# First token half ahead in the last two units of a stage, and x turned block by block in banks of its own

## Chip, cores and metric

The kernel runs on one core of a Trainium2 chip. The metric is the device time of one execution in microseconds (us). Below PE is TensorE (PEld its weight loads), ACT is ScalarE, DVE is VectorE, SP is the engine that issues most DMAs, POOL is GpSimd.

## What is computed

Two transformer blocks on 256 tokens of width 1024, all in float32. The first: a SwiGLU FFN (width 2816), an RWKV-7 mixer with a pooling branch, a second SwiGLU FFN. The second: windowed and differential attention, cross attention on a memory of 256 rows, a squared-ReLU MLP (width 4096). Each stage takes a root-mean-square norm of x, works, and adds to x:

```
x = x + 0.5 * swiglu(rms_norm(x, ffn1_norm), ffn1_w_gate, ffn1_w_up, ffn1_w_down)
h = rms_norm(x, mix_norm); p = h @ w_in
x = x + concatenate([y_rw, y_pool], axis=-1) @ w_out
x = x + 0.5 * swiglu(rms_norm(x, ffn2_norm), ffn2_w_gate, ffn2_w_up, ffn2_w_down)
x = rms_norm(x, final_norm)
...attention on x and cross attention on x and mem, then the MLP, each added to x
```

## The kernel before

**Units.** Every weight matrix is read once, in 280 units of 128x1024 elements (512 KB), numbered from the start of the program. SP loads a unit into one of three `raw` slots. ACT rounds it to a high part `whi` (`split_hi`, L1149), DVE takes the rest `wlo` (`split_lo`, L1652), each in a ring of six slots; a unit's slot is free when PE has used the unit of six before (`unit_used`). Activations are split in the same way, so PE multiplies high by high, high by low and low by high.

**Two kinds of unit.** `a_unit` produces a block of 128 outputs for all 256 tokens: for each of the 8 chunks c of the width it multiplies `XT[:, c]`, 512 columns (high and low) with `whi` and 256 with `wlo`. `b_half`, `b_unit` and `b_banks` produce 1024 outputs for 128 tokens (a token half, `tt` 0 or 1): 6 matmuls of 512 columns for one half, into banks 0 and 1 for the first half and 2 and 3 for the second. All go through the helper at L472. `b_last` is the last unit of a stage: first half, then second, with a signal (`quarter_used`) when each bank of 512 outputs is done.

**FFN.** 22 chunks of 128 hidden values. For chunk j PE computes a gate unit and an up unit (banks 4 and 6, or 5 and 7), ACT and DVE make H from them, and PE uses H in a down unit (`b_unit`). PE's order is gate and up of chunk j, then down of chunk j - 1. ACT and DVE go through `chunk(j)`, with three weight splits of later units woven in.

**A border between stages.** DVE adds the four banks to x (`update_x`, L1720 or L1722, one instruction for each quarter k: k is half and width half). PE turns x (`norm_t`, L561): 16 transposes of 128x128, two chunks of x to a bank, banks 4 to 7, in the order width half, token half. When both token halves of two chunks are there (`tp`), ACT scales and rounds them to `XT` high (`norm_hi`, L1186), then DVE takes the low part of both (`norm_lo`, L1696 and L1697) and signals `xt_ready`; the first `a_unit` of the next stage waits for `xt_ready` ahead of each second chunk. The norm itself (sum of squares, `norm_sums`, L1170, and the row scale by a matmul with a diagonal, `row_scale`) is applied later, to the outputs of the first units. Memory rows are turned in the last part of the second FFN (`norm_t("mem")`). A table of norm gains and other vectors comes in as rows, is turned by one matmul (L592) ahead of the last unit of the first FFN, and copied by DVE (L1827).

**Order.** The order of each engine's work is written out by hand; engines wait on semaphores that count events, and each engine runs its list strictly in order.

## Time and profile before

| | us |
|---|---|
| median of 3 runs | 994.62 |
| lowest, highest | 994.14, 995.46 |
| the profiled execution | 995.92 |
| its span (first to last instruction) | 994.0 |
| PE busy | 952.2 (96%) |
| PE weight loads busy | 817.2 (82%) |
| DVE busy | 664.2 (67%) |
| ACT busy | 541.2 (54%) |
| bytes read from HBM | 151.89 MB, mean 154 GB/s |

A row of the timeline gives start, duration, engine, line, operation, what is written from what, how many instructions are merged, and in brackets how long the engine was idle before and who released it. The stages are found by time: the first FFN to 202, the mixer to 373, the second FFN to 564, attention to 737, cross attention to 804, the MLP to the end.

### The profile page before, as it was taken

To read this page: it belongs to the slowest core of one execution; us is meant where nothing else is said; L and a number is where in the kernel's file an instruction comes from. 1 tells how busy PE (TensorE), PEld (TensorE's weight loads), DVE (VectorE), ACT (ScalarE), POOL (GpSimd) and SP (SyncE) were. 2 spreads that over 40 slices of the span, in tenths; PEclk is the share of its full clock that TensorE was granted. 3 is DMA by queue.
4 is the path that set the end of the run, shared out by engine and by line. 5 is a ranking of instruction groups with operands and counts; after the bars stand their busy time and mean duration, and the time that the engine had idled before them with its cause. 6 is when DMAs were issued, how large, how long until landed. Compare 5 with 4: busy or idle time off the path is not lost.

```text
span 994.0 us, 17685 instructions
## 1 busy us (share of the span) xinstructions
PE 952.2 (96%) x6228; PEld 817.2 (82%) x6228; DVE 664.2 (67%) x1101; ACT 541.2 (54%) x980; POOL 30.0 (3%) x59
## 2 busy tenths in 40 slices
PE   6999999989989999999999999998899999999997
PEld 5788888879889877888888887887888888888885
DVE  4776766577786467766667785777457366666665
ACT  6564555477545337555555676546646446554452
POOL 3002000000000001000000000002100000000000
PEclk9999999999999999999999999997999999999999
DMA  7677766545220226766656665552047136665652
GB/s 216 201 220 216 207 186 189 154 128 149 85 66 4 65 87 168 212 186 185 189 185 195 189 182 157 170 169 86 1 117 222 49 123 191 191 201 177 194 186 85
DMA packets 204177, 153.62 MB, mean 155 GB/s; under 512 B 5323, under 2 KB 189872, under 8 KB 204128
## 3 DMA queue, kind: packets, MB, share of 16 engines
q1 hardware_dynamic: 202896, 151.08, 50.9%
q0 software_dynamic: 1232, 1.87, 0.9%
q8 instruction: 32, 0.52, 0.2%
q14 instruction: 17, 0.14, 0.0%
HBM read 151.89 MB, written 1.05 MB: 154 GB/s over the span
## 4 chain that ended last, share of the span: by engine, by line
PE 84%; DVE 7%; ACT 5%; issue 2%; DMA 2%; SPq 0%; DVEq 0%; ACTq 0%
PE ps L472 83%; DVE wlo L1652 2%; ACT whi L1149 1%; DMA raw<-in_w_ckv 1%; DMA raw<-in_ffn_w_gate 1%; DVE XT L1697 1%; ACT XT L1186 0%; DMA raw<-in_w_up 0%; ACT arena L1358 0%; DVE X L1720 0%; ACT arena L1170 0%; DVE arena L1889 0%; PE ps L561 0%; DVE arena L1844 0%; ACT arena L1351 0%
## 5 line engine op out<-in xcount | busy, mean ns | idle before, releaser
L472 PE MATMUL ps<-XT,whi 128*128 128x512 f32 (+1 forms) x1584 | 521.9, 382 | 7.5 <-DVE XT L1697 7.5
L1652 DVE TENSOR_TENSOR wlo<-raw,whi 128x1024 fp32r<-128x1024 f32 x280 | 337.1, 1222 | 107.6 <-ACT whi L1149 86.6
L472 PE MATMUL ps<-XT,wlo 128*128 128x256 f32 x1440 | 404.8, 281 | 0.0
L472 PEld LDWEIGHTS ps<-XT,whi 128*128 128x128 f32 x1584 | 289.9, 189 | 69.7 <-issue 7.6
L1149 ACT ACTIVATE whi<-raw 128x1024 fp32r<-128x1024 f32 x280 | 292.4, 1054 | 53.0 <-PE ps L472 21.1
L472 PEld LDWEIGHTS ps<-XT,wlo 128*128 128x128 f32 x1440 | 273.2, 190 | 3.2
L472 PE MATMUL ps<-whi,H 128*128 128x512 f32 x608 | 177.7, 393 | 2.8 <-issue 2.5
L472 PEld LDWEIGHTS ps<-whi,H 128*128 128x128 f32 x608 | 109.0, 188 | 26.0 <-issue 2.7
L472 PE MATMUL ps<-arena 64*64 64x64 f32 (+6 forms) x1576 | 99.6, 250 | 8.6 <-DVE arena L2185 2.0
L472 PEld LDWEIGHTS ps<-arena 64*64 64x64 f32 (+3 forms) x1576 | 91.1, 153 | 16.6 <-DVE arena L2185 2.9
L472 PE MATMUL ps<-wlo,H 128*128 128x512 f32 x304 | 95.6, 393 | 0.0
L472 PEld LDWEIGHTS ps<-wlo,H 128*128 128x128 f32 x304 | 57.1, 188 | 13.3
L472 PE MATMUL ps<-whi,XT 128*128 128x512 f32 x192 | 56.1, 400 | 0.3 <-DVE XT L1696 0.3
L1211 ACT ACTIVATE arena<-ps 128x256 f32<-128x256 f32 x44 | 16.7, 380 | 58.5 <-PE ps L472 58.5
L1221 ACT ACTIVATE arena<-ps 128x256 f32<-128x256 f32 x44 | 16.9, 384 | 48.8 <-PE ps L472 48.8
L472 PEld LDWEIGHTS ps<-whi,XT 128*128 128x128 f32 x192 | 35.4, 188 | 9.3 <-issue 1.6
L1229 ACT ACTIVATE H<-arena 128x256 fp32r<-128x256 f32 x44 | 18.4, 418 | 38.5 <-DVE arena L1797 38.5
L1261 ACT ACTIVATE arena<-ps 128x256 f32<-128x256 f32 x42 | 16.0, 380 | 41.5 <-PE ps L472 41.5
L1786 DVE TENSOR_TENSOR arena<-ps,arena 128x256 f32<-128x256 f32 x44 | 18.6, 423 | 28.0 <-ACT arena L1211 27.9
L1593 ACT ACTIVATE arena<-ps 128x256 f32<-128x256 f32 x32 | 12.2, 381 | 46.0 <-PE ps L472 46.0
L1800 DVE TENSOR_TENSOR H<-arena,H 128x256 fp32r<-128x256 f32 x44 | 18.7, 426 | 24.4 <-ACT H L1229 24.4
L1597 ACT ACTIVATE H<-arena 128x256 fp32r<-128x256 f32 x32 | 13.4, 418 | 35.4 <-DVE arena L2295 35.4
(255 smaller groups left out, 713.6 us busy)
## 6 DMA issues: line engine op xcount, KB each, us to landing
raw<-in_ffn_w_gate SPq DMA_DIRECT2D x44, 512.0 KB, 4.6
raw<-in_ffn_w_up SPq DMA_DIRECT2D x44, 512.0 KB, 3.9
raw<-in_ffn_w_down SPq DMA_DIRECT2D x44, 512.0 KB, 4.7
raw<-in_w_in SPq DMA_DIRECT2D x36, 512.0 KB, 3.9
raw<-in_w_up SPq DMA_DIRECT2D x32, 512.0 KB, 4.0
raw<-in_w_down SPq DMA_DIRECT2D x32, 512.0 KB, 4.6
raw<-in_w_out SPq DMA_DIRECT2D x16, 512.0 KB, 3.5
raw<-in_w_ckv SPq DMA_DIRECT2D x16, 512.0 KB, 4.6
```

The source lines that it names most:

```text
L472: return pe.matmul(o, st, mv, start=start, stop=stop, skip_group_check=True)
L1149: act.activation(whi[:, n % RING, :], raw[:, n % RAW, :], ACT.Copy).then_inc(hi_ready, 1)
L1211: act.activation(GL[:, q, :], PS[4 + q][:, T:2 * T], ACT.Copy).then_inc(g_low, 1)
L1221: act.activation(UL[:, q, :], PS[6 + q][:, T:2 * T], ACT.Copy).then_inc(u_low, 1)
L1229: act.activation(H[:, q, 0:T], HS[:, q, :], ACT.Copy).then_inc(h_hi, 1)
L1261: act.activation(dst[:, i % 2, :], bank[:, T:2 * T], ACT.Copy).then_inc(sem_low, 1)
L1593: act.activation(UL[:, q, :], PS[4 + q][:, T:2 * T], ACT.Copy).then_inc(r_low, 1)
L1597: act.activation(H[:, q, 0:T], HS[:, q, :], ACT.Copy).then_inc(r_hi, 1)
L1652: dve.tensor_tensor(wlo[:, n % RING, :], raw[:, n % RAW, :], whi[:, n % RING, :].bitcast(F32), sub).then_inc(lo_ready, 1)
L1697: return dve.scalar_tensor_tensor(XT[:, c, T:2 * T], ps, scale, hi, mul, sub)
L1786: dve.tensor_tensor(GS[:, q, :], PS[4 + q][:, 0:T], GL[:, q, :], add).then_inc(g_raw, 1)
L1800: dve.tensor_tensor(H[:, q, T:2 * T], HS[:, q, :], H[:, q, 0:T].bitcast(F32), sub).then_inc(h_ready, 1)
```

## The change

- **Last two units.** Where a stage ends with two down units n and n + 1, PE takes the first token half of n, the first half of n + 1 (`b_banks`, both quarters signalled), the second half of n, then the second half of n + 1. This is `last_two` at the end of attention and cross attention; the mixer's end had its halves in such an order already; the FFNs are rewritten by hand. In the FFNs gate and up of chunk 21 are moved ahead of the down unit of chunk 19, loads and splits follow that order, and H of chunk 21 goes to a third slot.
- **Turning.** `turn_x(name, 0)` makes the 8 transposes of the first token half between the second half of unit n and the second half of unit n + 1; `turn_x(name, 1)` makes the other 8 after the last unit. Each transpose has a wait of its own. Chunks 0 to 3 go to banks 4 to 7, chunks 4 and 5 to banks 0 and 1, chunks 6 and 7 to the upper halves of banks 0 and 1.
- **Copy and split** go chunk by chunk: ACT signals each chunk, DVE signals each, and PE's first unit waits for each. In the shared banks ACT waits for the transposes of both chunks, and for chunks 6 and 7 also until DVE has read chunk 4 and 5. This holds at the start of the kernel too. The memory rows and the turning ahead of attention (`turn_pairs`) keep the pairs.
- **DVE.** The copy of the vector table in the first FFN is moved ahead of the last two splits of `chunk(21)`, and the transpose that it waits for behind the first half of unit 65. At the mixer's end the X updates of the first half are moved ahead of two splits.

What it makes of the order. PE at the end of attention (`whi,XT` and `wlo,XT` are the down units, `CON,X` the transposes, `XT,whi` the first unit of cross attention), before:

```order
L472 MATMUL ps<-whi,XT 128x512 x3
L472 MATMUL ps<-wlo,XT 128x512
L472 MATMUL ps<-whi,XT 128x512 x2
L472 MATMUL ps<-wlo,XT 128x512
L472 MATMUL ps<-whi,XT 128x512 x2
L472 MATMUL ps<-wlo,XT 128x512
L472 MATMUL ps<-whi,XT 128x512 x2
L472 MATMUL ps<-wlo,XT 128x512
L472 MATMUL ps<-whi,XT 128x512
L561 MATMUL ps<-CON,X 128x128 x16
L472 MATMUL ps<-XT,whi 128x512
```

and now:

```order
L486 MATMUL ps<-whi,XT 128x512 x3
L486 MATMUL ps<-wlo,XT 128x512 x2
L486 MATMUL ps<-whi,XT 128x512 x2
L568 MATMUL ps<-CON,X 128x128 x8
L486 MATMUL ps<-whi,XT 128x512
L486 MATMUL ps<-wlo,XT 128x512
L486 MATMUL ps<-whi,XT 128x512 x2
L486 MATMUL ps<-wlo,XT 128x512
L486 MATMUL ps<-whi,XT 128x512
L568 MATMUL ps<-CON,X 128x128 x8
L486 MATMUL ps<-XT,whi 128x512
```

Eight of the sixteen transposes now stand ahead of the last six matmuls. DVE at the end of the first FFN (`H` is the last chunk's, `wlo` the splits of two mixer units, `VEC` the table, `X` the updates), before:

```order
L1800 TENSOR_TENSOR H<-arena,H 128x256
L1652 TENSOR_TENSOR wlo<-raw,whi 128x1024 x2
L1827 COPY VEC<-ps 128x95
L1720 SCALAR_TENSOR_TENSOR X<-ps,SMALL,X 128x512 x4
L1697 SCALAR_TENSOR_TENSOR XT<-ps,VEC,XT 128x256 x8
```

and now:

```order
L1836 TENSOR_TENSOR H<-arena,H 128x256
L1843 COPY VEC<-ps 128x95
L1690 TENSOR_TENSOR wlo<-raw,whi 128x1024 x2
L1755 SCALAR_TENSOR_TENSOR X<-ps,SMALL,X 128x512 x4
L1735 SCALAR_TENSOR_TENSOR XT<-ps,VEC,XT 128x256 x8
```

The copy, which waits for PE, now stands ahead of both splits. DVE at the end of the mixer (numbers are the banks), before:

```order
L1652 TENSOR_TENSOR wlo<-raw,whi 128x1024 x4
L1722 TENSOR_TENSOR X<-ps0,X 128x512
L1722 TENSOR_TENSOR X<-ps1,X 128x512
L1722 TENSOR_TENSOR X<-ps2,X 128x512
L1722 TENSOR_TENSOR X<-ps3,X 128x512
```

and now:

```order
L1690 TENSOR_TENSOR wlo<-raw,whi 128x1024 x2
L1757 TENSOR_TENSOR X<-ps0,X 128x512
L1757 TENSOR_TENSOR X<-ps1,X 128x512
L1690 TENSOR_TENSOR wlo<-raw,whi 128x1024 x2
L1757 TENSOR_TENSOR X<-ps2,X 128x512
L1757 TENSOR_TENSOR X<-ps3,X 128x512
```

Two of the four splits now stand behind the updates of the first token half.

The core of the diff:

```diff
-        MEM_BANKS, T_BANKS = (4, 6, 5, 7), (4, 5, 6, 7)
+        PAIR_BANKS = {"mem": (4, 6, 5, 7), "mix2": (4, 5, 6, 7)}
+        X_BANKS = ((4, 0), (5, 0), (6, 0), (7, 0), (0, 0), (1, 0), (0, T), (1, T))
+
+        def turned_x(name, c):
+
+            if name in PAIR_BANKS:
+                bank, at = PAIR_BANKS[name][c // 2], (c % 2) * T
+            else:
+                bank, at = X_BANKS[c]
+            return PS[bank][:, at:at + T]
...
-                with sp.Fori(0, 10) as i:
+                with sp.Fori(0, 9) as i:
...
+                load(b + 57, 0, cols(u, 19 * P))
+                load(b + 58, 0, rows(d)[:, 18:19, :])
+                load(b + 59, 0, cols(g, 20 * P))
+                load(b + 60, 0, cols(u, 20 * P))
+                load(b + 61, 0, cols(g, 21 * P))
+                load(b + 62, 0, cols(u, 21 * P))
+                for j in (19, 20, 21):
+                    load(b + 44 + j, 0, rows(d)[:, j:j + 1, :])
...
-                    if after and c % 2 == 0:
-                        pe.wait_ge(xt_ready, 4 * NTP[after] + c // 2 + 1)
+                    if after:
+                        pe.wait_ge(xt_ready, KC * NTP[after] + (c - c % 2 + 2 if after in PAIR_BANKS else c + 1))
...
+            def turn_x(name, tt):
+
+                for c in range(KC):
+                    if name == "ffn1":
+                        pe.wait_ge(x_in[tt], 16)
+                    else:
+                        pe.wait_ge(x_upd, 4 * (UPD[name] - 1) + 2 * tt + c // 4 + 1)
+                    ins = pe.transpose(turned_x(name, c)[:, tt * P:(tt + 1) * P], X[:, tt, c * P:(c + 1) * P], ident)
+                    if tt == NT - 1:
+                        ins.then_inc(tp, 1)
+
+            def last_two(n, acts, name):
+
+                b_half(n, 0, acts[0], 0)
+                b_banks(n + 1, acts[1], 0, 2)
+                b_half(n, 0, acts[0], 1)
+                if name:
+                    turn_x(name, 0)
+                b_banks(n + 1, acts[1], 1, 1).then_inc(unit_used, 1)
+                if name:
+                    turn_x(name, 1)
...
-                with pe.Fori(0, 10) as i:
+                with pe.Fori(0, 9) as i:
                     for k in range(2):
                         gate_up(2 + k, 5 + 3 * k, i * 6, i * 2)
                         down(1 + k, 7 + 3 * k, i * 6, i * 2)
-                if f == 0:
+                gate_up(20, 59)
+                gate_up(21, 61)
+                down(19, 63)
+                pe.wait_ge(h_ready, J + 21)
+                if f:
+                    turn_pairs("mem", [0])
+                b_half(b + 64, 0, H[:, 0, :], 0)
+                pe.wait_ge(h_ready, J + FC)
+                b_banks(b + 65, H[:, 2, :], 0, 2)
+                if f:
+                    turn_pairs("mem", [1])
+                else:
                     pe.wait_ge(table_in, 16 * 4)
                     pe.wait_ge(rows_in, 16 * 17)
-                    pe.wait_ge(h_ready, FC)
                     pe.transpose(PS[7][:, KC:N_VEC], ROWS[0:N_VEC - KC, :],
                                  ident[0:N_VEC - KC, 0:N_VEC - KC]).then_inc(vec_tp, 1)
-                if f:
-                    norm_t("mem", [0])
-                    pe.wait_ge(h_ready, 2 * FC)
-                    norm_t("mem", [1])
-                pe.wait_ge(h_ready, J + FC)
-                b_last(b + 65, H[:, 21 % 2, :])
+                b_half(b + 64, 0, H[:, 0, :], 1)
+                if f == 0:
+                    pe.wait_ge(vec_ready, 2)
+                    turn_x("mix", 0)
+                b_banks(b + 65, H[:, 2, :], 1, 1).then_inc(unit_used, 1)
+                if f == 0:
+                    turn_x("mix", 1)
...
+                pe.wait_ge(yt_ready, 4 + 2)
+                for c in range(3):
+                    b_half(B_WOUT + 4 + c, 0, XT[:, c, :], 1)
+                turn_x("ffn2", 0)
+                b_banks(B_WOUT + 7, XT[:, 3, :], 1, 1).then_inc(unit_used, 1)
+                turn_x("ffn2", 1)
...
+                last_two(B_WOUT2 + KC - 2, [XT[:, c, :] for c in (KC - 2, KC - 1)], "cross")
...
             def norm_hi(name, gain):
-                q = NTP[name]
-                for b in range(4):
-                    act.wait_ge(tp, 4 * q + b + 1)
-                    for c in (2 * b, 2 * b + 1):
-                        bank = PS[(MEM_BANKS if name == "mem" else T_BANKS)[b]]
-                        ins = act.activation(XT[:, c, 0:T], bank[:, (c % 2) * T:(c % 2 + 1) * T], ACT.Copy,
-                            scale=vec(gain, c))
-                        if c % 2:
-                            ins.then_inc(xt_hi, 1)
+                q = KC * NTP[name]
+                for c in range(KC):
+                    if name in PAIR_BANKS:
+                        act.wait_ge(tp, q + c - c % 2 + 2)
+                    else:
+                        act.wait_ge(tp, q + (c + 1 if c < 4 else 7 + c % 2))
+                        if c >= 6:
+                            act.wait_ge(xt_ready, q + c - 1)
+                    act.activation(XT[:, c, 0:T], turned_x(name, c), ACT.Copy, scale=vec(gain, c)).then_inc(xt_hi, 1)
...
-                    n_gate, n_up = (0, 1) if j == 0 else (3 * j - 1, 3 * j)
+                    n_gate, n_up = (0, 1) if j == 0 else (61, 62) if j == 21 else (3 * j - 1, 3 * j)
+                    slot = 2 if j == 21 else q
...
             def norm_lo(name, gain):
-                q = NTP[name]
-                for b in range(4):
-                    dve.wait_ge(xt_hi, 4 * q + b + 1)
-                    for c in (2 * b, 2 * b + 1):
-                        bank = PS[(MEM_BANKS if name == "mem" else T_BANKS)[b]]
-                        ins = rest(c, bank[:, (c % 2) * T:(c % 2 + 1) * T], vec(gain, c))
-                    ins.then_inc(xt_ready, 1)
-
-            def update_x(nth, end, scale=0):
+                q = KC * NTP[name]
+                for c in range(KC):
+                    dve.wait_ge(xt_hi, q + (c - c % 2 + 2 if name in PAIR_BANKS else c + 1))
+                    rest(c, turned_x(name, c), vec(gain, c)).then_inc(xt_ready, 1)
+
+            def update_x(nth, end, scale=0, tiles=range(NT)):
 
                 if scale:
                     dve.wait_ge(fac_ready, scale)
-                for k in range(4):
+                for k in range(2 * tiles[0], 2 * tiles[-1] + 2):
...
+                        if f == 0:
+                            dve.wait_ge(vec_tp, 2)
+                            dve.tensor_copy(VEC[:, KC:N_VEC], PS[7][:, KC:N_VEC]).then_inc(vec_ready, 1)
...
-                for c in range(2, LEAD + 1 + KC - RING - 1):
-                    split_to(B_WOUT + RING + c + 1)
-                update_x(2, B_WOUT + KC)
+                split_to(B_WOUT + RING + 4)
+                update_x(2, B_WOUT + KC, tiles=[0])
+                split_to(B_WOUT + LEAD + KC)
+                update_x(2, B_WOUT + KC, tiles=[1])
```

## Rows read from the trace of the kernel before

**Rows 1.** The page, part 4: shares of the chain that ended last.
```profile
PE 84%; DVE 7%; ACT 5%; issue 2%; DMA 2%; SPq 0%; DVEq 0%; ACTq 0%
```

**Rows 2.** Timeline, attention to cross: start us, us, engine, line, operation, count [idle <-releaser].
```profile
736.65 0.39 PE L472 MATMUL ps<-whi,XT 128*128 128x512 f32 x1
...
736.88 1.91 PE L561 MATMUL ps<-CON,X 128*128 128x128 f32 x16
737.74 3.03 ACT L1186 ACTIVATE XT<-ps,VEC 128x256 fp32r<-128x256 f32 x8 [7.70 <-PE ps L561]
738.61 3.23 DVE L1697 SCALAR_TENSOR_TENSOR XT<-ps,VEC,XT 128x256 fp32r<-128x256 f32 x8 [0.84 <-ACT XT L1186]
...
739.63 0.47 PE L472 MATMUL ps<-XT,whi 128*128 128x512 f32 x1 [0.84 <-DVE XT L1697]
```

**Rows 3.** Timeline, first FFN to the mixer, PE and DVE.
```profile
198.99 0.24 PE L592 MATMUL ps<-CON,arena 95*128 95x95 f32 x1
...
199.18 2.36 DVE L1652 TENSOR_TENSOR wlo<-raw,whi 128x1024 fp32r<-128x1024 f32 x2 [0.45 <-PE ps L472]
...
201.63 2.72 DVE L1720 SCALAR_TENSOR_TENSOR X<-ps,SMALL,X 128x512 f32<-128x512 f32 x4
201.65 0.39 PE L472 MATMUL ps<-whi,H 128*128 128x512 f32 x1
...
206.39 0.47 PE L472 MATMUL ps<-XT,whi 128*128 128x256 f32 x2 [1.12 <-DVE XT L1697]
```

**Rows 4.** Timeline, mixer to the second FFN, PE and DVE.
```profile
369.81 2.59 DVE L1652 TENSOR_TENSOR wlo<-raw,whi 128x1024 fp32r<-128x1024 f32 x2 [2.75 <-ACT whi L1149]
...
372.32 0.39 PE L472 MATMUL ps<-whi,XT 128*128 128x512 f32 x1
...
376.90 0.47 PE L472 MATMUL ps<-XT,whi 128*128 128x512 f32 x1 [1.11 <-DVE XT L1697]
```

**Rows 5.** Timeline, start of the kernel, DVE, ACT and PE.
```profile
11.23 3.22 DVE L1697 SCALAR_TENSOR_TENSOR XT<-ps,VEC,XT 128x256 fp32r<-128x256 f32 x8
...
12.75 1.11 ACT L1149 ACTIVATE whi<-raw 128x1024 fp32r<-128x1024 f32 x1
...
22.07 1.06 ACT L1149 ACTIVATE whi<-raw 128x1024 fp32r<-128x1024 f32 x1 [1.65 <-DMA raw<-in_ffn_w_gate]
...
28.46 0.69 PE L472 MATMUL ps<-whi,H 128*128 128x512 f32 x2 [2.45 <-issue]
```

**Rows 6.** Timeline, the first H of the MLP, DVE and PE.
```profile
810.50 0.42 DVE L2293 TENSOR_TENSOR arena<-ps,arena 128x256 f32<-128x256 f32 x1 [0.33 <-ACT arena L1593]
...
811.93 0.43 DVE L2298 TENSOR_TENSOR H<-arena,H 128x256 fp32r<-128x256 f32 x1 [0.55 <-ACT H L1597]
...
812.71 0.63 PE L472 MATMUL ps<-whi,H 128*128 128x512 f32 x2
```

**Rows 7.** Timeline, the mixer's row scale, DVE and PE.
```profile
209.81 1.23 DVE L1652 TENSOR_TENSOR wlo<-raw,whi 128x1024 fp32r<-128x1024 f32 x1 [1.21 <-ACT whi L1149]
...
212.34 0.59 PE L472 MATMUL ps<-arena,SMALL 128*128 128x256 f32 x2
```

**Rows 8.** Timeline, end of the second FFN, DVE and PE.
```profile
559.03 0.43 DVE L1800 TENSOR_TENSOR H<-arena,H 128x256 fp32r<-128x256 f32 x1 [0.55 <-ACT H L1229]
...
560.99 0.48 PE L472 MATMUL ps<-whi,H 128*128 128x512 f32 x1
...
564.34 0.47 PE L472 MATMUL ps<-XT,whi 128*128 128x512 f32 x1 [0.35 <-DVE XT L1697]
```

**Rows 9.** Timeline, the first unit of the kernel, PE.
```profile
13.03 0.63 PE L472 MATMUL ps<-XT,whi 128*128 128x512 f32 x1
...
13.67 0.63 PE L472 MATMUL ps<-XT,whi 128*128 128x512 f32 x1
...
16.68 0.40 PE L472 MATMUL ps<-XT,whi 128*128 128x512 f32 x1
```

More of the change, by code:

```diff
@@ L492, in a_unit_summed @@
                 for c in range(KC):
-                    if after and c % 2 == 0:
-                        pe.wait_ge(xt_ready, 4 * NTP[after] + c // 2 + 1)
+                    if after:
+                        pe.wait_ge(xt_ready, KC * NTP[after] + (c - c % 2 + 2 if after in PAIR_BANKS else c + 1))
                     cs = slice(c * P, (c + 1) * P)
@@ L554, in norm_t @@
                             pe.wait_ge(mem_in, 16)
[L555 to L556 removed]
                         else:
                             pe.wait_ge(x_upd, 4 * (UPD[name] - 1) + 2 * tt + h + 1)
[L559 to L562 removed]
+                        for c in range(4 * h, 4 * h + 4):
+                            ins = pe.transpose(turned_x(name, c)[:, tt * P:(tt + 1) * P], src[:, tt, c * P:(c + 1) * P],
+                                               ident)
                             if tt == NT - 1:
[L564 removed]
+                                ins.then_inc(tp, 1)
             def ffn(b, f):
@@ L1045, in attention @@
                     last.then_inc(odt_mm, 1)
-                for c in range(KC):
+                for c in range(KC - 2):
                     pe.wait_ge(yt_ready, N_MIXED + max(4, c + 1))
-                    if c < KC - 1:
-                        b_unit(B_WOUT2 + c, 0, XT[:, c, :], start=(c == 0))
-                    else:
-                        b_last(B_WOUT2 + c, XT[:, c, :])
+                    b_unit(B_WOUT2 + c, 0, XT[:, c, :], start=(c == 0))
+                pe.wait_ge(yt_ready, N_MIXED + KC)
+                last_two(B_WOUT2 + KC - 2, [XT[:, c, :] for c in (KC - 2, KC - 1)], "cross")
             def cross():
-                norm_t("cross")
                 for i in range(KC):
@@ L1086, in cross @@
                 pe.wait_ge(sc_exp, 12 + 4)
-                for c in range(KC):
+                for c in range(KC - 2):
                     pe.wait_ge(yt_ready, N_MIXED + KC + c + 1)
-                    if c < KC - 1:
-                        b_unit(B_CO + c, 0, XT[:, c, :], start=(c == 0))
-                    else:
-                        b_last(B_CO + c, XT[:, c, :])
+                    b_unit(B_CO + c, 0, XT[:, c, :], start=(c == 0))
+                pe.wait_ge(yt_ready, N_MIXED + 2 * KC)
+                last_two(B_CO + KC - 2, [XT[:, c, :] for c in (KC - 2, KC - 1)], "mlp")
             def mlp():
```

38 lines of the change are left out of this document (8 added, 30 removed).

## The prediction

> **What bounds the kernel now.** I read the busy table and the chain of waits first: the chain lies 84% on PE and 83% on the one matmul helper, L472 [rows 1]. So the kernel is one row of matmuls, and what can be won is what stands between them where one stage ends and the next begins. I then read the timeline around each such border, engine by engine, because the chain merges the steps there. Three kinds of gap are seen. At the border from attention to cross attention PE issues its last matmul at 736.65 (done issuing .23 later, at 736.88), turns x with 16 transposes in 1.91, and issues the next matmul at 739.63: 2.75 us [rows 2]. From cross attention to the MLP the picture is the same. After the first FFN the same step takes 206.39 - 201.88 = 4.51 [rows 3], and after the mixer 376.90 - 372.55 = 4.35 [rows 4], because there the four X updates of DVE stand behind two weight splits (wlo). The start of the kernel has a wait of its own: PE idles 2.45 until 28.46, when the first H is ready [rows 5].
>
> **The new border, step by step.** Count from T, the end of the last matmul. Prices: an X update 2.72/4 = .68 [rows 3]; a copy of one chunk on ACT 3.03/8 = .38 in a row, .42 alone; a split of one chunk on DVE 3.23/8 = .40 [rows 2]; six matmuls of 512 columns 6 x .23 = 1.38 (736.65 to the next issue at 736.88) [rows 2]; eight transposes 1.91/2, so .9 without the tail [rows 2]. The sixteen transposes are no fewer, and eight of them now stand before the last six matmuls: T is .9 later. The third X update starts .19 after its quarter, which is three matmuls before T, and ends at T + .2. The first transpose of the second half goes at T + .27, ACT starts .29 later (rows 2: the sixth transpose, at 736.88 + 5 x .114 = 737.45, released ACT at 737.74), ends at T + 1.0; DVE, just through with its fourth update, splits chunk 0 until T + 1.4; PE starts at T + 1.5. Border: .9 + 1.5 = 2.4. Each transpose is now behind its own wait; the first of the sixteen stands behind one already met and follows at .23 like any other [rows 2], so I take 0 for them, and +.07 each, the lead an unhidden weight load could take, as no more than the upper end.
>
> **Attention to cross, cross to MLP.** The first matmul comes 2.75 - 2.4 = .35 earlier, but the first unit isn't bound by it. DVE hands over a chunk every .40 and PE uses it in .35 (a matmul of 512 columns at .23, one of 256 at half that), so the unit ends with DVE. Before: DVE starts at 738.61, ends 3.23 later, and PE has the two chunks of the last pair left: 738.61 + 3.23 + .06 + .70 = 742.60. Now: DVE starts at 736.88 + .9 + 1.0 = 738.78 and only one chunk is left behind it: 738.78 + 3.23 + .1 + .42 = 742.53. The .1 is the two last chunks, which share banks 0 and 1 with chunks 4 and 5, so ACT may take them only when DVE is done with those. I take **-.1** for each of the two (from -.4, if DVE gets ahead, to +.5 with the dear transposes).
> ACT ends its eight copies later, though: chunk 7 follows DVE's chunk 5, at 738.78 + 6 x .40 + .42 = 741.6 against 737.74 + 3.03 = 740.8. In the MLP ACT's next work is the hi split of a unit and DVE's the lo split behind it, and only then comes DVE's part of the first H, which had waited .33 for ACT at 810.50. H is ready there at 812.36 and PE takes it at 812.71 [rows 6], .35 of slack; DVE's three-step row (ACT 1.06, DVE 1.23) moves by .8 less that .3, so H comes at 812.9. PE waits **+.3** (0 to +.6).
>
> **Mixer to the second FFN.** Here the code does more: the first two X updates go ahead of DVE's last two splits (third pair of order excerpts), so they are over before unit 6 is. The splits end at 369.81 + 2.59 = 372.40 [rows 4], before the third quarter is ready at T - .69 = 372.76. So the border is the plain one, 2.4 for 4.35. In the unit's end: before, DVE started 1.02 before PE, as 738.61 stands before 739.63, at 375.88, unit end 375.88 + 3.23 + .76 = 379.87; now 372.55 + .9 + 1.0 = 374.45, end 374.45 + 3.23 + .1 + .42 = 378.20. **-1.7** (-2.0 to -1.2).
>
> **First FFN to the mixer.** Not so here. DVE's order is now H, VEC copy, two splits, X updates (second pair of excerpts). The copy waits for a transpose of the ROWS table that PE makes at 198.99 [rows 3] in both kernels, since the gate and up units and 24 down matmuls stand before it in both orders. Before, the splits ran from 199.18 and the copy after them; now DVE sits from its last H (some 3 us earlier, as chunk 21 is computed before unit 63) until 199.3, copies .25, splits 2.36 until 201.9 [rows 3], updates X until 202.6 and 203.3. PE is through with the half unit at 200.5 and stands: **the first turning waits for X, a new wait of 2.2 us**. Turning until 203.8, six matmuls: T = 205.2. DVE starts at T + 1.0 = 206.2 against 206.39 - 1.02 = 205.37, and the unit ends at 206.2 + 3.23 + .1 + .42 = 209.95 against 205.37 + 3.23 + .76 = 209.36: +.6. Then the row scale: PE made it at 212.34, after DVE's split at 209.81 (1.23) and .6 of scaling [rows 7], a slack of .7. This split waits for ACT, whose copies now end at 209.1 and no longer at 207.5: 1.6 later. xn so comes at 213.2 to 213.3. **+.9** (-.3, if DVE splits sooner than I think, to +1.4).
>
> **The start.** ACT went through its eight copies without DVE and began unit 1's hi split at 12.75; DVE began its chunks only at 11.23 [rows 5]. Now ACT's chunk 6 waits for DVE's chunk 4: 11.23 + 5 x .404 = 13.25, and the split follows at 14.0, 1.2 later. Behind it on ACT are the sums of squares, then splits 2 and 3; behind those on DVE the scale and lo splits; SP issues the next loads once these are done, and such a load is what ACT waited for at 22.07 (1.65) [rows 5]. The load ahead of it moves only .7, and if they share the way the delay is between .7 and 1.2. From there the first H hangs on ACT, and PE on H. PE's own start .4 earlier buys nothing, it only idles longer. **+1.0** (0, if loads and copies make it up, to +1.3).
>
> **Second FFN to the memory rows.** The turning of the memory rows has the same sixteen transposes, around another unit. H of chunk 21 was ready at 559.03 + .43 = 559.46 and PE took it at 560.99 [rows 8]. It hangs on a split and a load, so I don't let it move, while PE now wants it six matmuls and eight transposes earlier, at 560.99 - 1.38 - .8 = 558.8: a wait of .7. PE had waited .35 (.5 with the tail) for DVE at 564.34 [rows 8], which takes most of it, and the pace of DVE in that unit the rest. **+.1** (0 to +.7).
>
> **Sum.** -.1 -.1 +.3 -1.7 +.9 +1.0 +.1 = +.4 us. The profiled execution took 995.92 (span 994.0), so I expect 996.3 for one like it, and 994.62 + .4 = **995.0 for the median**; the profiled one stands 1.3 above that median with its recording, and the difference carries over.
>
> **Rivals.** (1) *The borders give what they seem to give.* If my two losses aren't there, because ACT and DVE make up for the bank waits and the splits run before the VEC copy is due, the gaps fall to 2.4 everywhere: -2.1, -1.95, -.35, -.35 = -4.75, so 989.9; with the DVE bound on the first unit kept and only the start and the first border free, -1.7 -1.4 -.2 = -3.3, 991.3. For it: 4.51 and 4.35 are real gaps [rows 3, 4]. Against: the order on DVE and the late start of its chunks at 11.23 [rows 5]. I give 15%.
> (2) *Slower, by the clock.* The wait before the first down unit grows from 2.45 to some 3.9 (mine plus the .4 of PE's earlier end). After 2.45 it held: the two matmuls at 28.46 take .69 together [rows 5], hardly more than two at full clock. If it falls to its lower level (1.2 for 2.4 GHz) there, the matmuls run as at the start, one chunk in .64 (13.03 to 13.67) for .35, until 16.68 [rows 9]: 3.65 x (1 - .35/.64) = 1.65, with the first chunk 1.8. Time 996.8. It decides only if the idle stretch is long enough, and my +1.0 comes with it. 10%.
> The Trainium skill, TensorE: Matmul & The Clock Gate, section on HAM oscillation, says that PE gaps beyond a certain length re-throttle the array and the ramp is paid again; by that page the longer wait is nearer to such a fall than the old one, and no row here shows a fall at this place.
> (3) *More waits of the small kind*: the dear transposes at all four borders (up to .07 x 16 each) and H late in both FFNs: +2 to +3, 997.2. 5%.
>
> **How the numbers follow.** Forecast, 70%: 995.0, own range 993.4 to 996.4 (the bounds of the terms don't all fall on one side). Rival 1 15%, rival 2 10%, rival 3 5%. For 8 in 10 the range goes to 992.3 below and 996.9 above. A measurement of this kernel can tell about 0.2%, here 2 us, from no change: faster means below 992.6, slower above 996.6. Faster: 13%, from rival 1 mostly. Slower: 12%, from rivals 2 and 3 and the forecast's edge. Same: 75%.
>
> **What would show it.** After the mixer: PE's gap made of eight transposes, six matmuls, eight transposes and .6 idle, the next stage 1.7 earlier. After the first FFN: PE idle for 2 us ahead of the first eight transposes, released by an X update; xn after 213. At the start: ACT waiting inside its eight copies for DVE, and PE idle for over 3 us before the first down unit at 29.4. At the two late borders: no more than .4 between old and new. Wrong it would be if PE doesn't wait for X after the first FFN, if the first H comes at 28.5 as before, or if the time is under 992.6.

## The result: about 0.3% slower

The changed kernel took 999.36 us (median of 5 executions, 999.01 to 1000.24), the kernel before 994.71 beside it (5 executions, 994.14 to 998.8): ratio 1.0033, 95% interval 1.002 to 1.0046. (The ratio is the estimate that goes with this interval; the two medians by themselves stand 1.0047 apart.) I had forecast 995.0 (992.3 to 996.9) and no change that can be told. The profiled execution of the changed kernel has a span of 997.6 us, that of before 994.0.

The chain of the changed kernel still lies on PE, 83% for 84% [rows 1]. So the 3.55 us between the two spans are to be found as steps between the same instructions of the two timelines. First the start, which answers to [rows 5]. Timeline, ACT, then PE (start us, us, engine, line, operation, count [idle <-releaser]; the helper of L472 is now L486, the copies of ACT L1226 for L1186, its hi split L1186 for L1149):

```profile
12.97 0.87 ACT L1226 ACTIVATE XT<-ps,VEC 128x256 fp32r<-128x256 f32 x2 [1.20 <-DVE XT L1735]
13.73 1.05 ACT L1186 ACTIVATE whi<-raw 128x1024 fp32r<-128x1024 f32 x1
...
22.54 1.06 ACT L1186 ACTIVATE whi<-raw 128x1024 fp32r<-128x1024 f32 x1 [1.68 <-DMA raw<-in_ffn_w_gate]
...
28.93 0.71 PE L486 MATMUL ps<-whi,H 128*128 128x512 f32 x2 [3.35 <-issue]
29.47 0.62 PE L486 MATMUL ps<-wlo,H 128*128 128x512 f32 x2
29.93 1.80 PE L486 MATMUL ps<-whi,H 128*128 128x512 f32 x4
31.53 1.05 PE L486 MATMUL ps<-wlo,H 128*128 128x512 f32 x2
```

ACT waits 1.20 for DVE ahead of its last two copies, the hi split comes at 13.73 for 12.75, and the first down unit (the first that uses H) .47 later, though the first load had landed .40 earlier here (DVE's first chunk 10.83 for 11.23): .87 counted from that load. Then four matmuls take 1.80. Busy time by windows, with the granted clock (PEclk), of the changed kernel and of before, shows why:

```profile
28.00:30.00 2.00, 1.07 (x5) 0.93 (x6) 1.15 (x2) 2.00 (x3) 0.00 (x0) 1.00 0.71 204
30.00:32.00 2.00, 2.00 (x7) 1.51 (x6) 1.97 (x3) 1.40 (x3) 0.00 (x0) 0.51 0.28 82
32.00:34.00 2.00, 2.00 (x8) 1.62 (x7) 1.96 (x4) 0.81 (x3) 0.00 (x0) 0.64 0.91 269
```
```profile
30.00:32.00 2.00, 2.00 (x12) 1.69 (x11) 1.97 (x5) 1.33 (x3) 0.00 (x0) 1.00 0.22 58
32.00:34.00 2.00, 2.00 (x13) 1.72 (x13) 1.86 (x3) 0.49 (x2) 0.00 (x0) 1.00 1.02 278
```

The third number from the right is the clock: 1.00 is 2.4 GHz, .5 is 1.2 GHz. It fell behind the wait of 3.35, at 30.0, when PE had been back at work for 1.1 us, and not behind 2.45. By 201.01, where the ROWS table is turned (198.99 before), the changed kernel is 2.02 behind: 1.55 of it for the fall.

Next the first FFN to the mixer [rows 3, 7], DVE, PE and DVE again:

```profile
197.55 0.42 DVE L1836 TENSOR_TENSOR H<-arena,H 128x256 fp32r<-128x256 f32 x1 [0.55 <-ACT H L1267]
201.29 0.26 DVE L1843 COPY VEC<-ps 128x95 f32<-128x95 f32 x1 [3.32 <-PE ps L634]
201.47 2.35 DVE L1690 TENSOR_TENSOR wlo<-raw,whi 128x1024 fp32r<-128x1024 f32 x2
203.73 1.40 DVE L1755 SCALAR_TENSOR_TENSOR X<-ps,SMALL,X 128x512 f32<-128x512 f32 x2
204.62 1.22 PE L568 MATMUL ps<-CON,X 128*128 128x128 f32 x8 [1.94 <-DVE X L1755]
...
209.02 0.47 PE L486 MATMUL ps<-XT,whi 128*128 128x256 f32 x2 [0.28 <-DVE XT L1735]
...
213.75 1.23 DVE L1690 TENSOR_TENSOR wlo<-raw,whi 128x1024 fp32r<-128x1024 f32 x1 [1.83 <-ACT whi L1186]
```

DVE stands 3.32 us for the table, PE 1.94 for X. And the mixer to the second FFN [rows 4], the one border that gained:

```profile
376.34 1.37 DVE L1757 TENSOR_TENSOR X<-ps,X 128x512 f32<-128x512 f32 x2
377.08 1.33 PE L568 MATMUL ps<-CON,X 128*128 128x128 f32 x8
...
378.59 0.47 PE L486 MATMUL ps<-XT,whi 128*128 128x512 f32 x1 [0.17 <-DVE XT L1735]
```

The whole way, as steps of the changed kernel against before (us, from the two profiles):

| stretch | step | forecast |
|---|---|---|
| first load lands | -.40 | - |
| start to the first H | +.86 | +1.0 |
| clock falls behind it | +1.55 | 0 |
| first FFN to mixer: first matmul +.61, row scale +.76 | +1.37 | +.9 |
| mixer to second FFN: first matmul -1.69, first unit +.31 | -1.38 | -1.7 |
| second FFN to memory -.10, and the rows behind -.26 | -.36 | +.1 |
| attention | -.83 | 0 |
| attention to cross: first matmul -.09, first unit +.30, behind it +.06 | +.27 | -.1 |
| clock falls in cross attention | +1.63 | 0 |
| cross to MLP: first matmul -.08, first unit +.31, first H another +.22, second H +.42 | +.87 | +.2 |

At the borders to the second FFN, to cross attention and to the MLP the first unit behind the border is .30 or .31 longer. ACT and DVE of the changed kernel at attention to cross show where from; PE starts the unit there at 740.35:

```profile
739.21 2.30 ACT L1226 ACTIVATE XT<-ps,VEC 128x256 fp32r<-128x256 f32 x6 [8.37 <-PE ps L568]
739.72 2.44 DVE L1735 SCALAR_TENSOR_TENSOR XT<-ps,VEC,XT 128x256 fp32r<-128x256 f32 x6 [0.25 <-ACT XT L1226]
741.87 0.87 ACT L1226 ACTIVATE XT<-ps,VEC 128x256 fp32r<-128x256 f32 x2 [0.35 <-DVE XT L1735]
742.37 0.88 DVE L1735 SCALAR_TENSOR_TENSOR XT<-ps,VEC,XT 128x256 fp32r<-128x256 f32 x2 [0.21 <-ACT XT L1226]
```

ACT waits .35 for DVE ahead of chunks 6 and 7, which share banks with 4 and 5, and DVE then .21 for ACT, so PE gets its last two chunks later.

The second fall of the clock stands where the two kernels do the same work behind the same wait (2.54 us in both). Timeline, PE, of the changed kernel: small matmuls go from .39 to .64 for two, and back.

```profile
773.76 0.39 PE L486 MATMUL ps<-LWG,arena 128*128 128x128 f32 x2
773.99 0.48 PE L486 MATMUL ps<-WPL,arena 128*128 128x128 f32 x2
774.26 0.64 PE L486 MATMUL ps<-LWG,arena 128*128 128x128 f32 x2
...
777.25 0.53 PE L486 MATMUL ps<-WPL,arena 128*128 128x128 f32 x2
777.62 0.39 PE L486 MATMUL ps<-LWG,arena 128*128 128x128 f32 x2
```

In attention the clock is low in both kernels (small matmuls), from 685.4 for 6.8 us here and from 682.0 for 10.2 before, and .83 was won there. (The clock isn't all of it: the changed kernel's second profile, below, won .56 with low stretches as long as before's.) So of 3.55 us, 1.63 are steps of the change's own (the six rows that have a forecast other than 0). The other 1.9 are the two falls, +3.18, less the .83 in attention and the .40 of the first load. Does that second part belong to the change?

### The profile page after: what moved, and what is told of

It reads as the page before. It is cut to its first block, busy times and chain, and to the rows that moved or that the text cites. A ratio compares the mean times of both kernels' runs of the same rounds, so it can differ in the third digit from the quotient of the medians.

```text
span 997.6 us, 17635 instructions
## 1 busy us (share of the span) xinstructions
PE 956.7 (96%) x6228; PEld 818.2 (82%) x6228; DVE 665.3 (67%) x1101; ACT 541.6 (54%) x980; POOL 30.0 (3%) x59
## 4 chain that ended last, share of the span: by engine, by line
PE 83%; DVE 7%; ACT 5%; issue 2%; DMA 2%; SPq 0%; DVEq 0%; ACTq 0%
PE ps L486 82%; DVE wlo L1690 2%; ACT whi L1186 1%; DVE XT L1735 1%; DMA raw<-in_w_ckv 1%; DMA raw<-in_ffn_w_gate 1%; PE ps L568 1%; ACT XT L1226 0%; DMA raw<-in_w_co 0%; DMA raw<-in_w_up 0%; ACT arena L1396 0%; ACT arena L1207 0%; DVE arena L1925 0%; DVE X L1755 0%; DVE arena L1880 0%
## 5 line engine op out<-in xcount | busy, mean ns | idle before, releaser
L486 PE MATMUL ps<-XT,whi 128*128 128x512 f32 (+1 forms) x1584 | 522.4, 382 | 4.7 <-DVE XT L1735 4.4
L486 PE MATMUL ps<-XT,wlo 128*128 128x256 f32 x1440 | 404.9, 281 | 0.0
L486 PEld LDWEIGHTS ps<-XT,whi 128*128 128x128 f32 x1584 | 290.2, 190 | 67.4 <-issue 3.7
L1186 ACT ACTIVATE whi<-raw 128x1024 fp32r<-128x1024 f32 x280 | 292.4, 1053 | 54.4 <-PE ps L486 20.8
L486 PEld LDWEIGHTS ps<-XT,wlo 128*128 128x128 f32 x1440 | 273.5, 190 | 3.2
L486 PE MATMUL ps<-whi,H 128*128 128x512 f32 x608 | 179.4, 395 | 4.2 <-issue 3.3
L486 PEld LDWEIGHTS ps<-whi,H 128*128 128x128 f32 x608 | 109.5, 189 | 28.2 <-issue 3.6
L486 PE MATMUL ps<-arena 64*64 64x64 f32 (+6 forms) x1576 | 99.0, 249 | 9.3 <-DVE arena L2222 2.6
L486 PEld LDWEIGHTS ps<-arena 64*64 64x64 f32 (+3 forms) x1576 | 90.1, 152 | 17.6 <-DVE arena L2222 4.0
L486 PE MATMUL ps<-wlo,H 128*128 128x512 f32 x304 | 96.1, 394 | 0.0
L486 PEld LDWEIGHTS ps<-wlo,H 128*128 128x128 f32 x304 | 57.3, 189 | 13.5
L486 PE MATMUL ps<-whi,XT 128*128 128x512 f32 x192 | 56.9, 401 | 0.3 <-DVE XT L1734 0.3
L486 PEld LDWEIGHTS ps<-whi,XT 128*128 128x128 f32 x192 | 35.4, 188 | 9.2 <-issue 1.6
L1267 ACT ACTIVATE H<-arena 128x256 fp32r<-128x256 f32 x44 | 18.4, 418 | 38.1 <-DVE arena L1832 38.1
L1226 ACT ACTIVATE XT<-ps,VEC 128x256 fp32r<-128x256 f32 x56 | 21.9, 482 | 22.5 <-PE ps L568 18.9
```

The costliest lines, as they stand in the source:

```text
L486: return pe.matmul(o, st, mv, start=start, stop=stop, skip_group_check=True)
L1186: act.activation(whi[:, n % RING, :], raw[:, n % RAW, :], ACT.Copy).then_inc(hi_ready, 1)
L1226: act.activation(XT[:, c, 0:T], turned_x(name, c), ACT.Copy, scale=vec(gain, c)).then_inc(xt_hi, 1)
L1267: act.activation(H[:, slot, 0:T], HS[:, q, :], ACT.Copy).then_inc(h_hi, 1)
```

## Experiments

All kernels below are compared in the same way, step by step against the profile of before, and by time against executions of before on the same chip. Over three such sets before took 993.65 to 999.77 us, mean 996.29 in 91 executions (996.37, 995.89 and 996.82 by set): one kernel spreads over 6 us.

**The changed kernel again.** No edit.

> The changed kernel itself, a second profile. Two falls of TensorE's clock stand in its trace that the kernel before does not have: at 30 to 33 us, behind the longer wait for the first H, and at 774 to 777 us in cross attention, where work and wait are the same in both kernels (2.54 us idle ahead of the same 32 small matmuls). If both belong to the kernel, both come again, at the same places, and the span is 997.2 to 998.4. Rival: the falls are chance from one execution to the next; then one is missing here and the span is some 1.6 us shorter.

Median 998.46 (996.99 to 1001.53), ratio 1.0035 (1.002 to 1.005). The profiled span was 995.2: the first H came .80 late as before, behind a wait of 2.89, and the clock did not fall there. Windows of this profile:

```profile
30.00:32.00 2.00, 2.00 (x10) 1.66 (x9) 2.00 (x3) 1.40 (x3) 0.00 (x0) 1.00 0.37 107
...
773.00:775.00 2.00, 2.00 (x12) 2.00 (x11) 0.00 (x0) 0.61 (x2) 0.00 (x0) 0.50 0.00 0
```

The clock is full behind the first H; in cross attention it fell again. A fall at some 267 us, in the mixer, that both earlier profiles had is gone as well (1.49 us shorter there). So one kernel has a fall in one execution and not in another, the rival's side; the span is 2.4 us shorter and not 1.6, since two falls are missing. The other steps came again: +.61 at the first border, +.35 and +.52 at the first Hs of the second FFN and the MLP.

**The start in the old way**: `PAIR_BANKS` gets "ffn1", and

```
-            turn_x("ffn1", 0)
-            turn_x("ffn1", 1)
+            turn_pairs("ffn1")
```

> The start alone is turned in pairs of banks as before; the rest is the changed kernel. Theory A (the bank wait makes loads and H late, the longer idle makes the clock fall): PE idles 2.4 to 2.9 us ahead of the first down unit, the clock holds, time 2.2 to 2.6 us under the changed kernel, 996.8 to 997.2. Theory B (clock falls anyway): .9 under it, 998.5. The fall at 774 us in cross attention: if it hangs on when that stretch comes, it may go or stay, worth 1.7.

Median 997.64, ratio 1.0022 (1.0009 to 1.0035). The start is that of before to .06 us (hi split at 12.74, first down unit 28.51), so the .86 belongs to the start's new turning; the next run narrows it to the banks. It is also well outside chance: counted from ACT's first split, DVE begins the low half of the first H after 19.81 to 19.95 us in the five profiles with the new start and its banks, and after 18.67 to 19.20 in the six with the old start. But the clock fell:

```profile
28.51 0.70 PE L486 MATMUL ps<-whi,H 128*128 128x512 f32 x2 [2.83 <-issue]
29.05 0.80 PE L486 MATMUL ps<-wlo,H 128*128 128x512 f32 x2
29.65 1.91 PE L486 MATMUL ps<-whi,H 128*128 128x512 f32 x4
31.36 1.05 PE L486 MATMUL ps<-wlo,H 128*128 128x512 f32 x2
```

Theory A's chain from the bank wait to the fall doesn't hold in this plain form: the late H is the change's, the fall can come without it. In cross attention it held here. The mean, 997.73, is 1.1 under the changed kernel's (standard error .7): nearer to theory B's .9 than to theory A's 2.2 to 2.6, but not settled by time.

**Other banks for chunks 6 and 7.**

```
-        X_BANKS = (..., (0, 0), (1, 0), (0, T), (1, T))
+        X_BANKS = (..., (0, 0), (1, 0), (6, T), (7, T))
-                            act.wait_ge(xt_ready, q + c - 1)
+                            act.wait_ge(xt_ready, q + c - 3)
```

with ACT's chunks 2 and 3 waiting until chunks 6 and 7 are turned.

> Chunks 6 and 7 of the turned x go to the second halves of banks 6 and 7, not of 0 and 1, so ACT waits for DVE's chunks 2 and 3 (long done) and no longer for 4 and 5. Theory A, the bank wait is what costs: at the start ACT's hi split comes back to 12.4 to 12.8 us, the first down unit .87 earlier than in the changed kernel, the clock holds there (1.55 more), and each later border gives back .2 to .3, the MLP's H another .4: in all 3.3 to 4.2 us under the changed kernel, 995.2 to 996.1. Theory B, the clock falls at the start whatever the wait there is: only 1.7 to 2.6 under it. Theory C, ACT waits for DVE elsewhere instead: under 1 us.

Median 996.36, ratio 1.0002 (.9986 to 1.0018). ACT's wait at the start is .42 for 1.20, the first H and the first down unit come as in before (28.43), behind a wait of 2.24, with the clock full. So the .86 of the start is the wait for the shared banks. The row scale's step is .33 for .76, the second FFN's H .12 for .31, the MLP's .20 for .53. Mean 996.44 for 998.81 (standard error of each .5): 2.4 less. That is theory A in its mechanism, step by step, but not in size: it asked for 3.3 to 4.2, and theory B for 1.7 to 2.6. Not all terms vanish, and a fall at the start is worth 1.5 us only in the executions that have it.

**The splits ahead of the table copy.**

```
-                        if f == 0:
-                            dve.wait_ge(vec_tp, 2)
-                            dve.tensor_copy(VEC[:, KC:N_VEC], ...)
                         next_split(0)
                         next_split(1)
+                        if f == 0:
+                            dve.wait_ge(vec_tp, 2)
+                            dve.tensor_copy(VEC[:, KC:N_VEC], ...)
```

> In the first FFN DVE makes its last two weight splits ahead of the copy of the vector table, as before the change. Theory: the splits start 2 to 3 us earlier, the X updates are no longer queued behind them, PE's wait of 1.94 us ahead of the first eight transposes goes, the first matmul of the mixer comes 1.7 to 2.0 earlier, xn with it: 1.3 to 2.0 us under the changed kernel, 997.4 to 998.1. Rival: ACT's hi splits come late, so DVE waits for them and the X updates stay where they are: within .5 of the changed kernel. Rival 2: xn is bound by ACT's sums and the row scale keeps its place: .3 to .6 gained only.

Median 996.28, ratio 1.0003 (.9991 to 1.0016). Timeline, DVE and PE:

```profile
198.73 2.36 DVE L1690 TENSOR_TENSOR wlo<-raw,whi 128x1024 fp32r<-128x1024 f32 x2 [0.46 <-ACT whi L1186]
201.58 0.26 DVE L1845 COPY VEC<-ps 128x95 f32<-128x95 f32 x1 [0.49 <-PE ps L634]
201.75 1.40 DVE L1755 SCALAR_TENSOR_TENSOR X<-ps,SMALL,X 128x512 f32<-128x512 f32 x2
...
202.81 1.06 PE L568 MATMUL ps<-CON,X 128*128 128x128 f32 x8
```

The splits run in the time that DVE had stood idle, and PE's wait of 1.94 is gone. The mixer's first matmul steps -1.67 for +.61: 2.28 us for the place of one copy of .26. This was the largest single loss of the change, and more than the 1.7 to 2.0 that I had expected. The mean, 996.36, is 2.4 under the changed kernel's. It is no chance of one profile: counted from the gate and up units ahead of the border, the mixer's first matmul is .63 or .64 later than in before in all six profiles with the copy in front, and 1.64 or 1.65 earlier in the three with it behind.

**The two late borders in the old way**: their last two units and sixteen transposes as before.

```
-                last_two(B_CO + KC - 2, [...], "mlp")
+                b_unit(B_CO + KC - 2, 0, XT[:, KC - 2, :])
+                b_last(B_CO + KC - 1, XT[:, KC - 1, :])
+                turn_pairs("mlp")
```

> The two late borders (attention to cross attention, cross attention to MLP) are put back: last units in the old order, sixteen transposes behind them, pairs of banks; the rest is the changed kernel. Theory A (there X updates were never late, so turning half of x ahead of the last six matmuls only makes ACT and DVE start .7 later, which the first unit and the MLP's H pay): with all spans taken at the same falls of the clock the stretch from the first matmul of cross attention to the MLP's end gets .36 + .5 + .4 = 1.3 us shorter against the changed kernel, and the border itself neither gains nor loses more than .1. Theory B (the new order is at least as good there, as I predicted: -.1 each, +.3 for H): no more than .2 shorter.

Median 998.59, ratio 1.0021 (1.0006 to 1.0036), too near to the changed kernel to be told by time. In the steps: the units behind the first border take .37 more than in the profile of before, where the changed kernel took .71 (its second profile) and .36 (its first). Three later profiles with the old border show .37 or .38 too, the kernel before with one wait lengthened among them, and two (the kernels with filled waits) show none: that is the pace of the matmuls (six in 1.06 us for 1.04, with no wait between them) and chance. The rest of .71, .34, is the border. At the MLP: first matmul +.01, first H .00 for +.53, second +.10 for +.42 and +.26. From the first matmul of cross attention on, with the same fall in it, this kernel is .75 shorter than the first profile of the changed one and .93 shorter than the second; I had expected 1.3. Theory A, with its size overdrawn.

**One part alone, in the kernel before**: at the mixer's end, X updates split around DVE's last two splits, and half of x turned ahead of the last six matmuls.

> The kernel before with one part of the change alone: at the mixer's end two X updates ahead of the last two splits, half of x turned ahead of the last six matmuls, block by block. Theory A: the first matmul of the second FFN comes 1.7 to 2.2 us earlier, .4 of it is lost to the first H, and 1.3 to 1.8 us are left at the end: 994.6 to 995.1 beside a mean of 996.4. Rival: the loads behind take it all back within the second FFN: within .5 of before.

Median 995.39, ratio 1.0002 (.9987 to 1.0018), mean 995.92 for 995.89: by time this is the rival, not theory A. The border gave only -.75 and the first H took .26 of it back. The rows of ACT, DVE and PE there:

```profile
370.47 1.06 ACT L1177 ACTIVATE whi<-raw 128x1024 fp32r<-128x1024 f32 x1 [1.88 <-DMA raw<-in_ffn_w_up]
371.56 1.23 DVE L1680 TENSOR_TENSOR wlo<-raw,whi 128x1024 fp32r<-128x1024 f32 x1 [1.72 <-ACT whi L1177]
372.70 1.28 DVE L1747 TENSOR_TENSOR X<-ps,X 128x512 f32<-128x512 f32 x2
373.44 1.25 PE L563 MATMUL ps<-CON,X 128*128 128x128 f32 x8 [1.04 <-DVE X L1747]
```

The third and fourth updates are still queued behind a split, the split behind ACT, and ACT behind a load, which it waited for 1.88 here. PE waited 1.04 for X. In the other profiles with this order ACT waited for that load .89 at most, and the first matmul came 1.5 to 1.7 earlier: the gain goes with the load, though no run moved that load alone.

**The start's wait filled.** Twelve matmuls ahead of the first down unit of the changed kernel, whose results are overwritten:

```
+                if f == 0:
+                    for k in range(12):
+                        mm(PS[2][:, :], XT[:, k % KC, 0:P], XT[:, k % KC, :])
```

> The changed kernel with twelve more matmuls (512 columns, into a bank that is overwritten later) ahead of the wait for the first H, so that PE idles .5 to .9 us there and no longer 3.3. Theory P (at every stretch in which PE idles, the clock falls in some executions and holds in others, and the idle is its cause): the clock never falls at 29 to 33 us, the first down unit comes no later, and the mean time is .4 to 1.2 us under the changed kernel's. Rival 1: the fall has another cause and is still seen there. Rival 2: the matmuls delay the first down unit by over .2.

Median 998.72, ratio 1.0029 (1.0013 to 1.0044). In the profile PE waits .15, the clock holds behind the first H, the down unit comes some .1 later; but the clock fell at 362.7, at the mixer's end, for the first time in these profiles. The mean, 998.64 for 998.81, tells of no gain, though the mean granted clock was .989 for .987: inconclusive by time.

**The start's wait lengthened**, in the kernel before: six repeats of one DVE addition ahead of the first H.

> The kernel before with DVE kept busy some 3 us longer ahead of the first H, so that PE idles 5 to 6 us there for 2.45. Theory P: the clock falls behind it, the gate and up units behind the first down unit take 1.6 us longer, and the mean is 3 + 1.6 x (the share of executions in which it holds in before) = 3.8 to 4.6 us over before's. Rival (falls at this place are chance whatever the wait): clock may hold; 3 us over before's.

Median 999.88, ratio 1.0032 (1.0018 to 1.0047); mean 1000.30, which is 4.0 more than the mean of all executions of before and 3.5 more than that of the set beside it (996.82): in the range of theory P by the one, between it and the rival's 3 by the other. The granted clocks decide: .984 to .986 in nine of these ten executions, but in only 11 of the 91 of before. The longer wait does lower the clock. Timeline, PE:

```profile
30.77 1.19 PE L472 MATMUL ps<-whi,H 128*128 128x512 f32 x2 [5.39 <-issue]
31.76 1.05 PE L472 MATMUL ps<-wlo,H 128*128 128x512 f32 x2
32.62 1.91 PE L472 MATMUL ps<-whi,H 128*128 128x512 f32 x4
```

H is 2.48 late and the stretch behind it another 2.17 long: here the clock was low for 6.8 us, not 3.4, and it had fallen at 28.7, inside the wait.

**A version from these results**: start and late borders old, table copy behind the splits, banks 6 and 7.

> All that the first runs point to: start and the two late borders in the old way; in the first FFN the splits ahead of the table copy; the new order kept around the first FFN's end, the mixer's end and the memory rows, with chunks 6 and 7 in banks 6 and 7. Theory A: against before 0 at the start, -1.7 to -2.0 at the first matmul of the mixer, -2.6 to -2.9 by the second FFN's first H, -.2 at the memory rows, 0 behind: 4.3 to 5.0 us faster than before, 991.5 to 992.1 beside a mean of 996.4. Rival: a gain in front is taken back by loads or xn: 2 us faster or less.

Median 994.44 (990.31 to 995.81), ratio .998 (.9966 to .9993). Steps: first H +.13, mixer's first matmul -1.65, second FFN's first H -2.74 (1.66 of it a fall that is absent, so -1.1), memory rows -.45 and -.26. That is 3.3 us of its own, less than the 4.3 to 5.0 that I had read out of single profiles without taking the falls off. By time it is less still: the mean is 993.87, 2.0 under the set of before beside it (2.4 under all), the most that the rival allowed, and far from the 991.5 to 992.1 of theory A.

**The same with its waits filled** (nine matmuls ahead of the first H, ten ahead of the small ones in cross attention), **and before with them.**

> The kernel of e6_best with matmuls that nothing needs put into the two idle stretches of PE behind which the clock fell in most profiles: nine ahead of the first H, ten ahead of the small matmuls in cross attention. Theory P (idle PE is what lets the clock fall there; nine profiles without such matmuls fell 5 times at the first place, at waits of 2.83 and more, and 6 of ten at the second): neither place falls, the stretch behind each is 1.6 us shorter than where it fell, and the mean is 1 to 2 us under e6_best's 993.9. Rival: the falls move to other places and the mean stays.

Median 992.44 (6 executions, 990.34 to 993.72), ratio .9953 (.9935 to .9971). Timeline, PE:

```profile
765.51 2.65 PE L486 MATMUL ps<-XT 128*128 128x512 f32 x10
768.67 0.49 PE L486 MATMUL ps<-LWG,arena 128*128 128x128 f32 x2 [0.52 <-DVE WPL L2313]
768.99 0.39 PE L486 MATMUL ps<-WPL,arena 128*128 128x128 f32 x2
```

> The kernel before with the same matmuls in the same two places. Theory P: no fall at either place, mean .7 to 1.5 us under before's 996.1. Rival: no less than before.

Median 995.49, ratio .9991 (.9978 to 1.0003), mean 995.52 for 996.29. In both profiles the clock held at both places. Together they speak for theory P: against the same kernels without the fills the means are -1.5 and -.8, each some two standard errors from nothing (-2.5 and -1.3 if each is first taken against the executions of before beside it; the two kernels of the first pair ran on different chips). In the second the clock fell at 360 us instead, as with the filled start above, so part of the rival stands too; the first has a fall at 264, where before has its own at 265.6.

Over all profiles the wait ahead of the first H and what came behind it are: 1.85, 2.24, 2.45 held; 2.83 fell; 2.89 held; 3.12, 3.16, 3.35, 3.76 and 5.39 fell; filled (0 to .42) held three times. In cross attention, with 2.53 to 2.92 us of wait: fell six times, held five; filled, held twice. Nor does a fall keep to one moment: behind the first H's wait it came between 2.1 us ahead of PE's return to work and 1.5 us after it.

## Why the prediction was wrong

Two steps of the prediction failed. The sum had the first units and the Hs behind the borders too cheap or at nothing, so the change's own steps are +1.6 and not +.4; and the clock was taken as held where it falls in a share of the executions. Beside them the base was too low by 1.7.

**The sum.** Point by point:
- *Start*, +1.0 forecast, +.86 measured: right in mechanism and size; putting back the start alone removed it, and so did other banks.
- *First FFN to the mixer*, +.9, measured +1.37. The new wait of PE for X was forecast at 2.2 and was 1.94. Mis-sized was what comes behind: I had the unit's end +.6; its first matmul alone is +.61 late and the bank wait adds .34 more, and another .42 comes behind the second unit, where PE takes the row scale.
- *Mixer to the second FFN*, -1.7, measured -1.38. The -1.7 was for the end of the first unit, with the first matmul 1.95 earlier; it came 1.69 earlier, and the unit, which ends with DVE, took .31 more than before. H adds nothing to that. What failed is the same as at the next border.
- *Second FFN to memory* [rows 8], +.1, measured -.36. PE did wait for H one step earlier, inside its first banks (three matmuls in 1.24 us at 560.39: a wait of .4 for the .7 forecast), but DVE's pace took it up as I said; the memory rows themselves were .26 shorter, which I had not looked for.
- *Attention to cross* [rows 2], -.1, measured about +.25 (-.09 and +.34). T came .88 later, as I said, but ACT began at T + .63, DVE at T + 1.14 and PE at T + 1.77, for my .56, 1.0 and 1.5, so the first matmul won .09 and not .35. Then I had DVE paced at .40 with one .1 for the banks: measured were .35 idle on ACT and .21 on DVE ahead of the last two chunks, and DVE ended its eight in 3.53 for 3.33. With the other banks the first unit's +.30 fell to +.12, with the old border to 0. The dear transposes (+.07 each) weren't there: the first eight took 1.03.
- *Cross to MLP* [rows 6], +.2 in sum, measured +.87: "PE waits +.3" for the first H was .53, and the second H's +.42 (+.26 in the second profile) was not in the sum at all. ACT's copies start some .7 later at a border where X was never late, its next split 1.2 later where I had .8 (811.73 for 807.79, less the 2.71 of the stages before), and its splits, loads and both H's follow.

Rival 1 (faster) failed for the reason that I had given against it: the two losses, at the start and after the first FFN, were there. Taking the largest out by moving one copy brought the kernel back to before's time.

**The clock.** Rival 2 named the place, the price (1.65 to 1.8; 1.55 to 1.63 measured) and the mechanism, and had 10%. The failed step is "after 2.45 it held": I took one execution's clock for the kernel's. In executions of one and the same kernel the fall comes and goes, so a sum wants a share of 1.6 us at each place where falls are seen, not a chance of all or nothing. That the rival's number came near is in part luck: its wait of 3.9 was 3.35 and 2.89 (PE didn't reach it earlier, counted from the first load), and in one of the two profiles the clock held. By the Trainium skill (TensorE: Matmul & The Clock Gate, the section on HAM oscillation), gaps beyond a certain length re-throttle the array. The runs agree in direction: the fall came behind every wait of 3.12 or more, the wait of 5.39 lowered the clock of nine executions in ten, and filling the wait kept it; that it held behind 2.89 and fell behind 2.83 shows that the length alone doesn't decide. The fall in cross attention, behind the same 2.54 in both kernels, is no part of the change.

**The base.** I put +.4 on a median of three executions, 994.62. The 91 later ones have a mean of 996.29, so 1.7 of the miss is the base; with it even the sum of +.4 gives 996.7. The ratios (1.0033, then 1.0035) don't hang on that: with 996.3 they say +3.3 to +3.5. The means say less: 999.04 in the 15 executions of the changed kernel, 2.75 above before's (standard error .4), and 2.4 for the second set against its own neighbours. Of this the change's own steps are 1.6.

For the rest the granted clock gives an estimate. The mean over executions is .9872 for the changed kernel and .9882 for before, and among the 91 executions of before a clock lower by .001 goes with .66 us more. That makes some .6 us of falls, and leaves .5 that is within chance. But before itself stood at .9878, .9890 and .9875 in its three sets, so the share of the longer wait can't be told from chance. That part stays open. So does this: the steps, read against one profile of before, promise more than time gives in each kernel with several new borders. They add up to +1.6, -.65 (splits ahead of the copy) and -3.3 (the version from the results), where the means stand at +2.4 to +2.75, 0 and -2.0 to -2.4.

## What to carry to other kernels

Turning half of the next input ahead of the last matmuls pays only where the next stage waits for something that this brings forward; where it doesn't, it starts ACT and DVE later, and their weight splits pass that on to the first two results of the next stage. When a queue is reordered, look at what stands at its head with a wait for another engine: here a copy of .26 us put ahead of two splits cost 2.3. And before a few tenths of a per cent are explained from two profiles, list where the clock was low in each and take that off; each fall here was worth as much as a whole border. A base wants many executions too: three of a kernel that spreads over 6 us were 1.7 us off.

## What I had not expected of the hardware

- The clock falls at the same place in one execution and not in another, with the same instructions and the same wait (2.53 or 2.54 us in cross attention: it fell in five profiles and held in three). Where it fell, at the start, in the mixer and in cross attention, it was low for 3.4 us (6.8 behind the wait of 5.39), which cost 1.5 to 1.66.
- Filling an idle stretch with matmuls that nothing needs kept the clock at that place in all five cases (three at the first, two at the second); the first down unit came .3 later in one of them. The fastest kernel here, .47% faster than before, has both fills; the fills alone, put into before, gave a ratio of .9991, which can't be told from no change.
- The same row of matmuls in cross attention ran at 1.04 us for six in five profiles and 1.06 in eight, .34 us over the stage's units, with nothing waiting and the clock at 1.00 in both.
